# An expert layer's start and its tail: lists from TensorE, throttled table scatters, fewer shuffles

## The reference

```python
u2 = rms_norm(h, norm_ffn_g)                     # 512 x 1024
logits = u2 @ router_w + router_b                # 32 experts
top_val, top_idx = lax.top_k(logits, 4); gates = softmax(top_val)
for e in range(32):                              # each token goes through its 4 experts
    hcat = xb @ w1[e] + b1[e]                    # 1024 -> 2048
    g, l = split(hcat); g = minimum(g, 7); l = clip(l, -7, 7)
    y = (g * sigmoid(1.702 * g) * (l + 1)) @ w2[e] + b2[e]
h = h + sum_k gates[n, k] * y[n, k]
out = rms_norm(h, final_norm_g)
```

## Time and profile before

| | |
|---|---|
| time before, median of 3 runs | 1569.45 us (1568.13 to 1570.44) |
| the profiled execution | 1571.4 us, its span 1569.7 us |
| TensorE products busy | 1535.4 us, 98% |
| weight loads of TensorE (PEld) | 902.1 us, 57% |
| VectorE | 746.2 us, 48% |
| GpSimd | 528.1 us, 34% |
| ScalarE | 282.6 us, 18% |
| DMA, mean over the span | 314 GB/s, 492.24 MB |

### The profile page before, as it was taken

The page is one execution under the profiler, slowest core; times in us unless marked ns, Lnnn a source line. Parts: engine busy times, 40 slices in busy tenths (PEclk is TensorE's granted clock), DMA queues, the critical chain, the costliest instruction groups (busy, mean ns, idle before and its releaser), DMA issues.

```text
span 1569.7 us, 37658 instructions
## 1 busy us (share of the span) xinstructions
PE 1535.4 (98%) x15984; PEld 902.1 (57%) x15984; DVE 746.2 (48%) x1579; ACT 282.6 (18%) x406; POOL 528.1 (34%) x682
## 2 busy tenths in 40 slices
PE   6999999999999999999999999999999999999996
PEld 6998998877889646443344334434443443344334
DVE  4799899115233633443353334334433443353358
ACT  5333133356222300100010001000100100010001
POOL 7333433463334435322222222222223222222225
PEclk9999999999999999999999999999999999999998
DMA  7553144221175389999999999999999999999994
GB/s 221 162 169 127 57 147 121 81 81 54 59 303 218 95 285 426 423 425 426 426 424 424 426 420 426 425 420 424 423 419 424 423 427 419 424 426 424 427 420 195
DMA packets 103539, 492.24 MB, mean 314 GB/s; under 512 B 12309, under 2 KB 70569, under 8 KB 78404
## 3 DMA queue, kind: packets, MB, share of 16 engines
q1 hardware_dynamic: 83732, 463.29, 73.0%
q0 software_dynamic: 10128, 17.25, 3.0%
q10 hardware_dynamic: 9632, 11.03, 2.3%
HBM read 475.46 MB, written 24.87 MB: 319 GB/s over the span
## 4 chain that ended last, share of the span: by engine, by line
PE 93%; DVE 3%; POOL 1%; issue 1%; SPq 1%; ACT 1%; DMA 1%; another core or an unknown queue 0%; DVEq 0%; POOLq 0%; ACTq 0%
PE banks L1624 42%; PE banks L1161 28%; PE banks L1653 20%; DVE h_res L2194 1%; DMA stage<-in_w_in_dram 1%; SPq L464 0%; PE banks L1520 0%; PE banks L1393 0%; POOL w_lo L627 0%; POOL w_lo L636 0%; DVE u L1977 0%; PE banks L1294 0%; SPq L450 0%; ACT w_hi L868 0%; DVE h_res L2203 0%
## 5 line engine op out<-in xcount | busy, mean ns | idle before, releaser
L1624 PE MATMUL banks<-w_ring,xT 128*32 128x512 f32 x6144 | 670.6, 592 | 1.4 <-issue 1.0
L1624 PEld LDWEIGHTS banks<-w_ring,xT 128*32 128x32 f32 x6144 | 216.7, 110 | 434.5 <-issue 420.9
L1653 PE MATMUL banks<-w_ring,actT 128*32 128x256 f32 x6144 | 339.7, 379 | 0.2 <-issue 0.2
L1653 PEld LDWEIGHTS banks<-w_ring,actT 128*32 128x32 f32 x6144 | 210.8, 110 | 135.3 <-issue 18.0
L2118 DVE TENSOR_TENSOR hid<-banks,bias_now 128x512 f32<-128x512 f32 x96 | 63.9, 666 | 470.3 <-PE banks L1624 470.3
L636 POOL TENSOR_TENSOR w_lo<-stage,w_hi 128x2048 fp32r<-128x2048 f32 x38 | 175.4, 4615 | 257.9 <-ACT w_hi L868 257.9
L695 POOL TENSOR_TENSOR carrier<-carrier 1x1 f32<-1x1 f32 x161 | 30.9, 193 | 590.4 <-DVE y_out L2147 404.2
L1135 ACT ACTIVATE sig<-hid 128x256 f32<-128x256 f32 x96 | 40.0, 417 | 905.1 <-DVE hid L2119 905.1
L1161 PE MATMUL banks<-u_hi,w_hi 128*128 128x264 f32 (+1 forms) x528 | 176.7, 335 | 0.9 <-POOL w_lo L627 0.9
L1161 PE MATMUL banks<-u_hi,w_lo 128*128 128x264 f32 (+1 forms) x528 | 175.2, 332 | 0.0
L1161 PE MATMUL banks<-u_lo,w_hi 128*128 128x264 f32 (+1 forms) x528 | 174.8, 331 | 0.0
(11 more groups left out here) (307 smaller groups left out, 1451.0 us busy)
## 6 DMA issues: line engine op xcount, KB each, us to landing
w_ring<-in_expert_w_dram SPq DMA_DIRECT2D x192, 2048.0 KB
stage<-in_w_in_dram SPq DMA_DIRECT2D x20, 1024.0 KB, 5.2
stage<-in_w_in_dram SPq DMA_DIRECT2D x16, 512.0 KB, 5.6
y_rows<-empty_row ACTq DMA_DIRECT2D x8, 1024.0 KB, 4.7
y_in<-y_rows SPq DMA_DIRECT2D x4, 2048.0 KB, 17.4
stage<-in_conv_pw_w_dram SPq DMA_DIRECT2D x4, 1024.0 KB, 5.2
stage<-in_mlstm_out_w_dram SPq DMA_DIRECT2D x4, 1024.0 KB, 5.2
stage<-in_w_out_dram SPq DMA_DIRECT2D x4, 1024.0 KB, 5.5
```

What stands on the lines that cost most here:

```text
L1624: last = nc.tensor.matmul(banks[32 * g:32 * (g + 1), t].rearrange("p (c j) -> p c j", j=128), xT[:, t, k], units, start=k == 0, stop=k == ...
L1653: last = nc.tensor.matmul(banks[32 * g:32 * (g + 1), 3 + t, 0:GRP], actT[:, t, k], w2_ring[k // 4][:, k % 4, GRP * g:GRP * (g + 1)], start ...
```

## The change

It removes the four scatters that follow each of tiles 0 and 1, and sends all sixteen later: three, five and five behind the three row requests of expert 1, which now wait for row_turn as those of later experts do, and the last three behind the first request of expert 2. A scatter waits for the one three before it (three semaphores). VectorE makes slot columns of expert 2 as well (in_third) and, for each token, the code of its assignment to expert 0 (first_code); TensorE multiplies both (eight products more), and VectorE writes from these the piece lists of experts 1 and 2 and the row list of expert 0. So expert 0's results and expert 2's rows no longer wait for the table. The table is read into 32 partitions in place of four copies: first the part of the first pass, after all scatters, then the rest, behind expert 1's results; the lists are written once for each of four groups of partitions. In the tail, the shuffle of the second bias and the turning of the biases go ahead of the last expert, the shuffle of the first bias takes the place of the second's within it, GpSimd multiplies tile 3 alone, and VectorE scales tiles 2, 1 and 0.

```diff
@@ -42,7 +42,7 @@
-EARLY = 4
+IN_FLIGHT = 3
...
-SCALED_BY_POOL = (3, 2)
+SCALED_BY_POOL = (3,)
...
@@ -669,7 +673,8 @@
             pool.wait_ge(mm_done, pair_tick(WO_PAIR + 1, 8))
             nc.gpsimd.memset(no_code, NONE).then_inc(moe_consts, 1)
             nc.gpsimd.iota(code, [[TOPK * P, TT], [1, TOPK]], base=0, channel_multiplier=TOPK)
-            nc.gpsimd.iota(token_no, [[P, TT]], base=0, channel_multiplier=1, allow_small_or_imprecise_dtypes=True)
+            nc.gpsimd.iota(token_no, [[P, TT]], base=-NONE, channel_multiplier=1, allow_small_or_imprecise_dtypes=True)
+            nc.gpsimd.iota(code_no, [[TOPK * P, TT], [1, TOPK]], base=-NONE, channel_multiplier=TOPK, allow_small_or_imprecise_dtypes=True)
             nc.gpsimd.iota(expert_id, [[1, NE]], base=0, channel_multiplier=0, allow_small_or_imprecise_dtypes=True)
             nc.gpsimd.memset(all_ones, 1.0)
...
             chain(nc.gpsimd.iota(steps96, [[SLOTS, PASSES - 1]], base=SLOTS, channel_multiplier=0, allow_small_or_imprecise_dtypes=True))
-            for g in range(CG):
-                chain(nc.gpsimd.memset(group_of[32 * g:32 * (g + 1)], float(g)))
...
@@ -694,7 +697,7 @@
                 nc.gpsimd.tensor_tensor(carrier[:, 1 + i:2 + i], carrier[:, 0:1], carrier[:, 0:1], ALU.add).then_inc(idx_step, 1)
-            def request_rows(turn=None):
+            def request_rows(turn=None, between=None):
                 carry_wait(0)
...
-
-            def gather(n, copied, turn=None):
+                    if between is not None:
+                        places_out(between[t])
+
+            def gather(n, copied, turn=None, between=None):
                 nc.gpsimd.tensor_copy(piece_now, piece_of[:, :, bass.ds(n, 1)].rearrange("p t o -> p (t o)")).then_inc(idx_step, 1)
                 pool.wait_ge(idx_step, copied)
-                request_rows(turn)
+                request_rows(turn, between)
...
-            def places_out(i):
-
-                pool.wait_ge(dest_made, i + 1)
-                for m in range(TOPK * i, TOPK * (i + 1)):
+            def places_out(columns):
+
+                for m in columns:
+                    pool.wait_ge(dest_made, m // TOPK + 1)
+                    if m >= IN_FLIGHT:
+                        pool.wait_ge(table_written[m % IN_FLIGHT], 16 * (m // IN_FLIGHT))
                     pool.indirect_dma_start(out=table, out_offset=bass.IndirectOffsetOnAxis(ap=dest[:, m:m + 1], axis=0),
-                                            in_=code[:, m:m + 1], in_offset=None).then_inc(table_written, 16)
-
-            pool.wait_ge(table_set, 16)
-            for i in range(2):
-                places_out(i)
-
-            for i in range(TT):
-                pool.wait_ge(u2_stored[i], 16)
-            pool.wait_ge(tables_made, CG * TG)
-            pool.sem_inc(idx_step, 1)
-            request_rows()
-            for i in range(2, TT):
-                places_out(i)
-
-            pool.wait_ge(table_written, 16 * TT * TOPK)
-            for g in range(CG):
-                pool.dma_start(code_of[32 * g:32 * (g + 1)], table.rearrange("(x j e) o -> j x (e o)", j=32, e=NE)).then_inc(rows_in, 16)
-            pool.wait_ge(rows_in, 16 * CG)
-            def lists_of(codes, tokens, pieces, rows):
-
-                chain(nc.gpsimd.tensor_scalar(tokens, codes, -1.5, 0.25, ALU.add, ALU.mult))
-                chain(nc.gpsimd.tensor_scalar(tokens, tokens, TO_WHOLE, None, ALU.add))
-                chain(nc.gpsimd.tensor_scalar(tokens, tokens, -TO_WHOLE, None, ALU.add))
-                nc.gpsimd.tensor_scalar(pieces, tokens, float(CG), group_of, ALU.mult, ALU.add)
-                chain(nc.gpsimd.tensor_scalar(rows, codes, float(CG), group_of, ALU.mult, ALU.add))
-
-            def results_out(n, stored):
+                                            in_=code[:, m:m + 1], in_offset=None).then_inc(table_written[m % IN_FLIGHT], 16)
+
+            def results_out(n, stored, meanwhile=None):
...
+                if meanwhile is not None:
+                    meanwhile()
                 pool.wait_ge(y_stored, stored * (16 * TG))
                 carry_wait(1 + TG)
-            lists_of(code_of[:, 0:TG, 0:EARLY], token_part[:, 0:TG, 0:EARLY], piece_of[:, :, 0:EARLY], row_of[:, :, 0:EARLY])
+            codes_of_slot = table.rearrange("(x j e) o -> j x (e o)", j=32, e=NE)
+
+            def tokens_of(tokens, codes):
+
+                chain(nc.gpsimd.tensor_scalar(tokens, codes, -1.5, 0.25, ALU.add, ALU.mult))
+                chain(nc.gpsimd.tensor_scalar(tokens, tokens, TO_WHOLE, None, ALU.add))
+                chain(nc.gpsimd.tensor_scalar(tokens, tokens, -TO_WHOLE, None, ALU.add))
+
+            def lists_of(g, tokens, codes, pieces, rows):
+
+                nc.gpsimd.tensor_scalar(pieces, tokens, float(CG), float(g), ALU.mult, ALU.add)
+                chain(nc.gpsimd.tensor_scalar(rows, codes, float(CG), float(g), ALU.mult, ALU.add))
+
+            def later_codes_in():
+
+                pool.dma_start(code_of[:, TG:PASSES * TG], codes_of_slot[:, TG:PASSES * TG]).then_inc(rows_in, 16)
+
+            pool.wait_ge(table_set, 16)
+            for i in range(TT):
+                pool.wait_ge(u2_stored[i], 16)
+            pool.wait_ge(tables_made, CG * TG)
+            gather(1, 1, 1, (range(0, 3), range(3, 8), range(8, 13)))
+            pool.wait_ge(tables_made, 2 * CG * TG)
             nc.gpsimd.tensor_copy(row_now, row_of[:, :, 0]).then_inc(idx_step, 1)
             pool.wait_ge(idx_step, 3 + TG)
             pool.wait_ge(y_emptied, 16 * KT)
             results_out(0, 1)
             pool.wait_ge(xT_made, 2 * TG)
-            gather(2, 8 + TG, 2)
+            gather(2, 8 + TG, 2, (range(13, 16), (), ()))
+
+            for i in range(IN_FLIGHT):
+                pool.wait_ge(table_written[i], 16 * len(range(i, TT * TOPK, IN_FLIGHT)))
+            pool.dma_start(code_of[:, 0:TG], codes_of_slot[:, 0:TG]).then_inc(rows_in, 16)
+            pool.wait_ge(rows_in, 16)
+            tokens_of(token_part[:, 0:TG], code_of[:, 0:TG])
+            for g in range(CG):
+                lists_of(g, token_part[:, 0:TG], code_of[:, 0:TG], piece_of[32 * g:32 * (g + 1), :, 0:NE], row_of[32 * g:32 * (g + 1), :, 0:NE])
+            nc.gpsimd.tensor_copy(row_now, row_of[:, :, 1]).then_inc(idx_step, 1)
+            pool.wait_ge(idx_step, IDX + 3 + TG)
+            results_out(1, 2, later_codes_in)
+            pool.wait_ge(xT_made, 3 * TG)
+            gather(3, IDX + 8 + TG, 3)
+            pool.wait_ge(rows_in, 32)
             for t in range(TG):
-                lists_of(code_of[:, t::TG], token_part, piece_of[:, t, 0:PASSES * NE].rearrange("p (q e) -> p q e", e=NE),
-                         row_of[:, t, 0:PASSES * NE].rearrange("p (q e) -> p q e", e=NE))
+                tokens_of(token_part[:, 1:PASSES], code_of[:, TG + t::TG])
+                for g in range(CG):
+                    lists_of(g, token_part[:, 1:PASSES], code_of[:, TG + t::TG],
+                             piece_of[32 * g:32 * (g + 1), t, NE:PASSES * NE].rearrange("p (q e) -> p q e", e=NE),
+                             row_of[32 * g:32 * (g + 1), t, NE:PASSES * NE].rearrange("p (q e) -> p q e", e=NE))
             pool.dma_start(last_g, final_norm_g.rearrange("(a d) -> a d", a=1).to_broadcast([P, D])).then_inc(last_g_in, 16)
             pool.wait_ge(passes_made, 1)
             passes = pool.value_load(n_passes[0:1, 0:1], min_val=1, max_val=PASSES)
             first_expert = pool.alloc_register("first_expert")
-            pool.reg_mov(first_expert, 1)
+            pool.reg_mov(first_expert, 2)
...
-            def last_root(m):
-
-                i = TILE_ORDER[2 + m]
-                pool.wait_ge(squared, before + 4 + m + 1)
+            def last_root(m, count):
+
+                i = TILE_ORDER[m]
+                pool.wait_ge(squared, before + count)
                 rstd(P, f_square[:, i:i + 1], f_rstd[:, i:i + 1], D, rstd_made)
-            for m, i in enumerate(TILE_ORDER[:2]):
-                pool.wait_ge(squared, before + m + 1)
-                rstd(P, f_square[:, i:i + 1], f_rstd[:, i:i + 1], D, rstd_made)
+            last_root(0, 1)
+            pool.wait_ge(squared, before + 2)
             pool.wait_ge(last_g_in, 16)
-            for m, i in enumerate(SCALED_BY_POOL):
-                pool.wait_ge(squared, before + 2 + m + 1)
-                nc.gpsimd.tensor_tensor(h_res[:, i], h_res[:, i], last_g, ALU.mult).then_inc(out_made_pool, 1)
-                if m == 0:
-                    last_root(0)
-            last_root(1)
+            i = SCALED_BY_POOL[0]
+            nc.gpsimd.tensor_tensor(h_res[:, i], h_res[:, i], last_g, ALU.mult).then_inc(out_made_pool, 1)
+            for m in range(1, TT):
+                last_root(m, m + 2)
...
             for m in range(2):
                 last_square(m)
-            for m, i in enumerate(SCALED_BY_POOL):
-                act.wait_ge(rstd_made, CHUNKS + TT + m + 1)
```

(52 more changed lines are left out.)

14 lines of the change are left out of this document (9 added, 5 removed).

## The result

The changed kernel takes 1571.85 us in the median of 15 runs (1569.96 to 1576.80), the kernel before 1569.45 (1567.91 to 1571.33) beside it: a ratio of 1.0021, interval 1.0013 to 1.0028. It is slower by 2.4 us, where 5.6 us less were forecast. Seven of its 15 runs took 1573.9 to 1576.8 us and the other eight 1570.0 to 1571.9; the profile is one of the eight, so what the longer ones lose is not seen. The profiled execution of the changed kernel took 1570.9 us, its span is 1569.2.

A forecast was written before the change was run, and what follows sets the result against it. TensorE's expert products were taken to bound the kernel. Terms -2.6 + 1.4 - 4.0 - 0.2 (expert 1) - 0.2 (tail) = -5.6 us, from 1569.45 to 1563.9 us; range 1561.0 to 1572.0, the forecast's own 1561 to 1566.3.

The forecast's parts named there:

- before expert 0: First slot columns to expert 0: the 2.97 us stall goes (-2.6 us), added slot columns and products cost +1.4 us.
- the standstill: Expert 0: with at most three scatters open the long TensorE stop should not form, -4.0 of 5.0 us.
- the tail: After the last expert: shuffles leave, one GpSimd/VectorE collision goes, another comes; -0.2 us, bounds -1.65 and +0.2.
- the throttle: GpSimd's queue in expert 0: waiting scatters cost nothing; expert 2's rows land at 58 to 59 us, needed at 62.
- the lists: GpSimd in expert 2: list building grows by 7 us for three tiles, hidden where it waits for results anyway.
- the late GpSimd: Rival, TensorE waits for rows before experts 2 to 4: no loss to 7.5 us scatter latency, 10 us at 10; chance 0.07.
- the widest range I named: Whole kernel: 1561.0 to 1572.0 us; the forecast's own range was 1561 to 1566.3.
- a row transposition waits past the end of an expert: Sign at the experts' ends that would show the forecast wrong; no size given.

The follow-up runs named there:

- lists split: Changed kernel with the late lists of the three tiles built one tile at a time in experts 2, 3 and 4: 0.9988 of the kernel before.
- six open: Changed kernel with six scatters open at once instead of three: 0.9999 of the kernel before.
- five open: Same as the best run with four open, but with five scatters open: 0.9995 of the kernel before.
- early requests: On top of lists split, three scatters open: expert 1's three row requests leave together ahead of scatters 3 to 12: 0.9994 of the kernel before.
- four open: Early requests with four scatters open, expert 2's requests early, full products ahead of expert 0, no GpSimd product in tail: 1565.2 us, 0.9969 of before.
- the tail alone: Kernel before with only the tail's part of the change: 0.9993 of the kernel before.

## Why the prediction was wrong

**Right: before expert 0.** The stall of 2.97 us went and the work added cost 1.3 us: -1.5 us against -1.2. **Right: the standstill.** First products of expert 0 are 22.3 us instead of 25.0, and without the clock they would be 20.6: 4.4 us of standstill gone, 4.0 expected. The 36.37 and 31.34 us that I took 5.0 from go from piece to piece of the chain of waits; from first product to first product expert 0 lasted 35.41 us and expert 1 32.10, and 4.4 was all there was. That it is the crowd, and not a fixed price for each scatter, is shown for these products by six against three open. **Right: the tail.** -0.1 against -0.2, with the product inside the sums as described, and without it 1.6 us less.

**Wrong: the throttle and the lists at nothing.** This is the step that failed: "3 us to spare, no loss", and the lists "in expert 2, where it waits for results anyway". The pace of the throttle was right (8.8, 8.7 and 7.2 us for three scatters against 7.8; the last of the thirteen issued 38 us after expert 0's start against 36), and the results of expert 0 left 2.8 us after they were made, as foretold. But I followed one path only, that of the results to expert 2. The row request of tile 2 I named as standing behind the waiting scatters and never timed: it was due for expert 1, and TensorE stood 1.8 us for it in the changed kernel and 2.2 with the lists split. And the lists' added length was about right (15 us after 9.1, so 6 where I had 7), but not their cover: the last three scatters and the code load behind them had put the results of expert 1 and the requests of expert 3 at 612 to 628 (with six open it is no earlier), so that the list block ran into the results of expert 2. That cost 3.4 us at expert 4; splitting it gave them back.

**Not foreseen: the clock.** I took the added one-column products at the time of their instructions. They leave TensorE 2.7 us without a full product ahead of expert 0, and the clock it starts with is half: 1.7 us, which twelve full products among them took away. The same 1.7 us follow the stop before expert 4. Together that is more than the whole difference.

Of the rivals, the late GpSimd was right in kind and given 7 in 100; it was bound to a scatter's latency above 7.5 us, and came without it: the three that the chain of waits shows in expert 0 landed 6.4 to 7.0 us after their instruction ended. That the 1571.85 us lie inside the widest range I named (to 1572.0) is luck. By the signs I had named, "a row transposition waits past the end of an expert" is what the trace shows, twice.

By terms, from the second and third table columns of the result: -1.5 before expert 0, -0.3 +0.3 -0.4 +3.4 +1.7 in experts 0 to 4, -0.6 at the end, of which 0.5 lie behind the last operation and belong to no term; +2.6 by the traces, +2.4 by the times.

## What to carry to other kernels

When a throttle or a wait goes into an in-order queue, list everything that stands behind it up to the next time the queue is empty, with the moment each item is due; here both items that broke were others than the one the wait was reckoned for. Work "hidden in a wait" is hidden only as long as the queue arrives there early, so recompute the arrival after every other edit. And look at what a tensor engine does in the microseconds before a hot loop: a stretch of tiny products can cost as much again in the loop (1.7 us here) as they take themselves.

## What the hardware showed that I had not expected

The standstill has one form wherever it comes. In the kernel before, with six open and with five open TensorE starts a handful of products every 1.4 us (start, us, products):

```profile
558.95 1.06 PE banks L1624 x4
...
560.38 1.32 PE banks L1624 x4
...
561.80 1.31 PE banks L1624 x4
...
563.34 1.07 PE banks L1653 x4
...
564.79 1.09 PE banks L1653 x4
...
575.70 1.09 PE L1689 MATMUL banks<-w_ring,actT 128*32 128x256 f32 x5 [0.79 <-issue]
577.14 0.62 PE L1689 MATMUL banks<-w_ring,actT 128*32 128x256 f32 x3 [0.34 <-issue]
578.55 0.64 PE L1689 MATMUL banks<-w_ring,actT 128*32 128x256 f32 x4 [0.79 <-issue]
579.98 1.73 PE L1689 MATMUL banks<-w_ring,actT 128*32 128x256 f32 x27 [0.79 <-issue]
```

What holds TensorE then is open: its products wait for nothing that the trace shows, and the clock is 1.00. Idle transfer engines are not the cause: they finish nothing in the kernel before (share 0.00 at 561 to 563) and are busy with five open (0.77 to 1.17 from 574 to 580). Nor does the number of open scatters settle it alone: three cost nothing in the first products of expert 0 (20.6 us with the clock held up), and with the early requests some 4.7 us in the second products of expert 1. The best run, with four open, still takes 65.4 us for experts 0 and 1, where two undisturbed ones take 61.9.

An idle TensorE does not always lose its clock: in the changed kernel it stayed at 1.00 after the stop of 1.8 us before expert 1 and fell to 0.50 after the 2.5 us before expert 4; with the lists split it stayed at 1.00 after 2.2 us before expert 1.

The end of the span follows the last operation by 4.4 us with the tail alone, 3.9 in the changed kernel and 2.9 with the lists split, though the three have the same tail. No run here tells why.
